# One 256-column pass for each token's product in the table of weights, with the low part of u on GpSimd

## The reference, cut to what matters

```python
idx = jnp.take_along_axis(cand_i, pos, axis=-1)      # i1 * 128 + i2
gate = jax.nn.softmax(top_s, axis=-1)
hid = jnp.einsum('td,thkd->thk', xb, u_tab[ib]).astype(jnp.float32)
coef = (jax.nn.gelu(hid, approximate=False) * gb).astype(xb.dtype)
y = jnp.einsum('thk,thkd->td', coef, v_tab[ib])
```

## Time and profile before

| | before |
|---|---|
| median of 3 runs | 2252.08 us |
| profiled execution, in all | 2255.32 us |
| its span | 2253.5 us |
| TensorE busy | 2013.6 us (89%) |
| VectorE busy | 1570.8 us (70%) |
| ScalarE busy | 1002.6 us (44%) |
| GpSimd busy | 125.6 us (6%) |
| table stage | about 1630 to 1881 us of the span |
| expert stage | about 1882 to 2241 us |

### The profile page before, as it was taken

How to read it: one execution, slowest core, us unless ns; L and a number is a source line. 1 busy time by engine, 2 the same in 40 slices (tenths; PEclk the granted TensorE clock), 3 DMA queues, 4 the chain that set the end, 5 groups by cost and what they waited for, 6 DMA issues and landing times. The chain is left out here.

```text
span 2253.5 us, 40848 instructions
## 1 busy us (share of the span) xinstructions
PE 2013.6 (89%) x16472; PEld 1805.2 (80%) x16472; DVE 1570.8 (70%) x2622; ACT 1002.6 (44%) x1669; POOL 125.6 (6%) x109
## 2 busy tenths in 40 slices
PE   8877799988779996998788888899899999999996
PEld 4875599968559894878777868899899998888885
DVE  3658778867559886776566565589977776667665
ACT  2515444335553343323344553445456665454453
POOL 1000000000230001530000300000000000000000
PEclk9967999989789998998899988999999999999998
DMA  7672578835137882314000025477555555777775
GB/s 262 229 165 82 196 291 319 310 119 187 59 134 282 304 299 70 119 57 151 1 4 4 2 86 189 150 230 216 181 170 176 176 176 196 240 242 244 241 241 179
DMA packets 185264, 393.24 MB, mean 174 GB/s; under 512 B 14826, under 2 KB 130154, under 8 KB 173546
## 3 DMA queue, kind: packets, MB, share of 16 engines
q1 hardware_dynamic: 166642, 373.83, 49.1%
q10 hardware_dynamic: 18434, 16.79, 2.2%
HBM read 371.17 MB, written 19.40 MB: 173 GB/s over the span
## 5 line engine op out<-in xcount | busy, mean ns | idle before, releaser
L1319 ACT CAST experts_v_hi<-peer_v 128x1024 fp32r<-128x1024 f32 x128 | 134.3, 1050 | 175.8 <-PE experts_py L1309 174.7
L1516 PE MATMUL ffn_pa<-all_h_hi,ffn_u_hi 128*128 128x256 f32 x704 | 199.4, 283 | 7.1 <-DVE ffn_u_lo L1581 7.0
L1305 PE MATMUL experts_py<-experts_v_hi,experts_c_hi 128*128 128x512 f32 x512 | 200.4, 391 | 5.3 <-DVE experts_c_lo L1350 5.3
L1306 PE MATMUL experts_py<-experts_v_lo,experts_c_hi 128*128 128x512 f32 x512 | 200.1, 391 | 0.0
L1517 PE MATMUL ffn_pa<-all_h_lo,ffn_u_hi 128*128 128x256 f32 x704 | 198.2, 282 | 0.0
L1518 PE MATMUL ffn_pa<-all_h_hi,ffn_u_lo 128*128 128x256 f32 x704 | 198.2, 281 | 0.0
L1309 PE MATMUL experts_py<-experts_v_hi,experts_c_lo 128*128 128x512 f32 x512 | 158.4, 391 | 0.0
L3148 PE MATMUL table_pa<-all_h_hi,table_u_hi 128*128 128x256 f32 x512 | 151.1, 295 | 7.6 <-DVE table_u_lo L3116 7.6
L1344 DVE TENSOR_TENSOR experts_v_lo<-peer_v,experts_v_hi 128x1024 fp32r<-128x1024 f32 x128 | 155.9, 1218 | 0.6 <-ACT experts_v_hi L1319 0.6
L3070 PE MATMUL route_pa<-all_h_hi,route_u_hi 128*128 128x256 f32 x512 | 146.5, 286 | 8.8 <-DVE route_u_lo L2955 8.8
L3071 PE MATMUL route_pa<-all_h_lo,route_u_hi 128*128 128x256 f32 x512 | 145.7, 285 | 0.0
(11 more groups left out here) (586 smaller groups left out, 5828.9 us busy)
## 6 DMA issues: line engine op xcount, KB each, us to landing
peer_v<-in_peer_v SPq DMA_DIRECT2D x128, 512.0 KB, 3.4
ffnw_u<-in_ffn_columns SPq DMA_DIRECT2D x44, 1024.0 KB, 7.9
ffn_ada_w<-in_ada_w SPq DMA_DIRECT2D x40, 1024.0 KB, 5.4
route_u<-in_peer_u SPq DMA_DIRECT2D x64, 512.0 KB, 3.8
table_u<-in_peer_u SPq DMA_DIRECT2D x64, 512.0 KB, 3.3
ffnw_v<-in_ffn_rows SPq DMA_DIRECT2D x44, 512.0 KB, 8.7
peer_kept<-hid_kept SPq DMA_DIRECT2D x128, 128.0 KB, 3.4
l1w_w<-in_diff_w_in SPq DMA_DIRECT2D x12, 1024.0 KB, 5.1
```

The lines of the kernel that those rows point to most:

```text
L1305: pe.matmul(py[:, 2 * t + n, :], c_hi[:, b, part], v_hi[:, r, cols], start=start, stop=False)
L1306: pe.matmul(py[:, 2 * t + n, :], c_hi[:, b, part], v_lo[:, r, cols], start=False, stop=False)
L1516: pe.matmul(out, u_hi[:, b, cols], h_hi[:, c, :], start=(c == 0), stop=False)
```

## The change

- `first` and `second` become float32r. The gates are rounded at the start of the stage to a high part; high part and remainder are kept in PSUM (`gates`). `second` gets 256 columns for each token: the one-hot row times the high part, and beside it times the low part. A token's product is one matmul of 256 columns, whose two halves are summed later.
- `one_hot` on VectorE is now: `equal` (comparison of the second keys, whole quad), `first` (the same for the first keys), `second` (a product of `equal` with the gates, 1024 elements).
- `products` goes by halves of a quad, with 5 PSUM banks for halves in place of 4 for quads. ScalarE copies the low half of each product into `table` (`low_table`), and VectorE adds the high half from PSUM (`store`), one step behind `one_hot`.
- `low_u` moves from VectorE to GpSimd.
- `table` lies as [key 1, token, key 2], so the copies write it densely, and `weigh` in `experts` reads it with a stride of 128 values.
- `hid` has 2 buffers in place of 3.

```diff
-                dve.tensor_tensor(coef[:, i % 2, :], feed_h.slot(i), table[:, i, :], ALU.mult).then_inc(weighed, 1)
+                dve.tensor_tensor(coef[:, i % 2, :], feed_h.slot(i), table[:, :, i], ALU.mult).then_inc(weighed, 1)
...
-    ring, hots, banks = 3, 2, 4
+    ring, kept, hots, banks = 3, 2, 2, 5
...
-        first = st.sb("first", [P, hots, per, NKEYS])
-        second = st.sb("second", [P, hots, per, NKEYS])
+        first = st.sb("first", [P, hots, per, NKEYS], F32R)
+        equal = st.sb("equal", [P, per, NKEYS])
+        second = st.sb("second", [P, hots, per, 2, NKEYS], F32R)
...
-        hid = st.sb("hid", [P, ring, S])
-        psum = st.ps("psum", [P, banks, CW])
+        hid = st.sb("hid", [P, kept, S])
+        psum = st.ps("psum", [P, banks, per // 2, 2, NKEYS])
+        gates = st.ps("gates", [P, 2, S])
...
+        @block.gpsimd
+        def _(pool):
+            for j in range(late):
+                pool.wait_ge(u_hi_ready, j + 1)
+                pool.tensor_tensor(u_lo[:, j % 2, :], u[:, j % ring, :], u_hi[:, j % 2, :].bitcast(F32), ALU.subtract
+                                   ).then_inc(u_split, 1)
...
             def one_hot(i):
                 b = i % hots
+                at = slice(i * per, (i + 1) * per)
+                keys = k["iota"][:].unsqueeze(1).broadcast_to(wide)
+                if i >= 1:
+                    dve.wait_ge(hot, i)
+                dve.tensor_tensor(equal[:], chosen[:, 1, at].unsqueeze(2).broadcast_to(wide), keys, ALU.is_equal
+                                  ).then_inc(equal_ready, 1)
                 if i >= hots:
-                    dve.wait_ge(product, i - hots + 1)
-                wide = [P, per, NKEYS]
-                at = slice(i * per, (i + 1) * per)
-                dve.tensor_tensor(first[:, b], chosen[:, 0, at].unsqueeze(2).broadcast_to(wide),
-                                  k["iota"][:].unsqueeze(1).broadcast_to(wide), ALU.is_equal)
-                for j in range(per):
-                    key, gate = [chosen[:, c, i * per + j:i * per + j + 1] for c in (1, 2)]
-                    last = dve.tensor_scalar(second[:, b, j, :], k["iota"][:], key, gate, ALU.is_equal, ALU.mult)
-                last.then_inc(hot, 1)
-
-            for i in range(max(late, quads)):
-                if i < late:
-                    low_u(i)
-                if i < quads:
-                    one_hot(i)
+                    dve.wait_ge(product, 2 * (i - hots + 1))
+                dve.tensor_tensor(first[:, b], chosen[:, 0, at].unsqueeze(2).broadcast_to(wide), keys, ALU.is_equal)
+                dve.wait_ge(equal_ready, i + 1)
+                dve.tensor_tensor(second[:, b], equal[:].unsqueeze(2).broadcast_to(pair),
+                                  gates[:, :, at].rearrange("p a t -> p t a").unsqueeze(3).broadcast_to(pair),
+                                  ALU.mult).then_inc(hot, 1)
+
+            def store(i):
+                for half in range(2):
+                    n = 2 * i + half
+                    dve.wait_ge(copied, n + 1)
+                    at = i * per + half * per // 2
+                    to = table[:, at:at + per // 2, :]
+                    dve.tensor_tensor(to, to, psum[:, n % banks, :, 0, :], ALU.add).then_inc(stored, 1)
+
+            high = second[:, 0].rearrange("p t a n -> p (t a n)")[:, 0:S]
+            dve.tensor_copy(high, chosen[:, 2, :]).then_inc(gate_ready, 1)
+            dve.wait_ge(gate_ready, 1)
+            dve.tensor_copy(gates[:, 0, :], high.bitcast(F32)).then_inc(gate_ready, 1)
+            dve.tensor_tensor(gates[:, 1, :], chosen[:, 2, :], high.bitcast(F32), ALU.subtract).then_inc(gate_ready, 1)
+            dve.wait_ge(gate_ready, 3)
+            for i in range(quads):
+                one_hot(i)
+                if i >= 1:
+                    store(i - 1)
+            store(quads - 1)
...
-                if i >= banks:
-                    pe.wait_ge(stored, i - banks + 1)
-                for j in range(per):
-                    last = pe.matmul(psum[:, i % banks, j * P:(j + 1) * P], first[:, b, j, :], second[:, b, j, :],
-                                     start=True, stop=True)
-                last.then_inc(product, 1)
+                for half in range(2):
+                    n = 2 * i + half
+                    if n >= banks:
+                        pe.wait_ge(stored, n - banks + 1)
+                    for m in range(per // 2):
+                        j = half * per // 2 + m
+                        last = pe.matmul(psum[:, n % banks, m].rearrange("p a n -> p (a n)"), first[:, b, j, :],
+                                         second[:, b, j].rearrange("p a n -> p (a n)"), start=True, stop=True)
+                    last.then_inc(product, 1)
...
-            def store(i):
-                act.wait_ge(product, i + 1)
-                act.copy(table[:, :, i * per:(i + 1) * per].rearrange("p n t -> p t n"),
-                         psum[:, i % banks, :].rearrange("p (t n) -> p t n", t=per)).then_inc(stored, 1)
+            def low_table(i):
+                for half in range(2):
+                    n = 2 * i + half
+                    at = i * per + half * per // 2
+                    act.wait_ge(product, n + 1)
+                    act.copy(table[:, at:at + per // 2, :], psum[:, n % banks, :, 1, :]).then_inc(copied, 1)
```

More of the change, by code:

```diff
@@ L3084, in peer_table @@
     late = columns.shape[0] - early
-    ring, hots, banks = 3, 2, 4
+    ring, kept, hots, banks = 3, 2, 2, 5
     h_hi, h_lo = k["h_hi"], k["h_lo"]
     with Stage(nc, "table") as st:
-        first = st.sb("first", [P, hots, per, NKEYS])
-        second = st.sb("second", [P, hots, per, NKEYS])
+        first = st.sb("first", [P, hots, per, NKEYS], F32R)
+        equal = st.sb("equal", [P, per, NKEYS])
+        second = st.sb("second", [P, hots, per, 2, NKEYS], F32R)
         u = st.sb("u", [P, ring, D])
         u_hi, u_lo = (st.sb(n, [P, 2, D], F32R) for n in ("u_hi", "u_lo"))
-        hid = st.sb("hid", [P, ring, S])
-        psum = st.ps("psum", [P, banks, CW])
+        hid = st.sb("hid", [P, kept, S])
+        psum = st.ps("psum", [P, banks, per // 2, 2, NKEYS])
+        gates = st.ps("gates", [P, 2, S])
         pa = st.ps("pa", [P, 2, CW])
         u_loaded = [st.sem(f"u_loaded{i}") for i in range(ring)]
-        hid_kept_done = [st.sem(f"hid_kept{i}") for i in range(ring)]
-        hot, product, stored, u_hi_ready, u_split, rows_ready, acted = (
-            st.sem(n) for n in ("hot", "product", "stored", "u_hi_ready", "u_split", "rows_ready", "acted"))
+        hid_kept_done = [st.sem(f"hid_kept{i}") for i in range(kept)]
+        gate_ready, equal_ready, hot, product, copied, stored, u_hi_ready, u_split, rows_ready, acted = (
+            st.sem(n) for n in ("gate_ready", "equal_ready", "hot", "product", "copied", "stored", "u_hi_ready", "u_split", "rows_ready", "acted"))
         block = st.block()
@@ L3108, in _ @@
                 feed.begin(sp)
-            for b in range(ring):
-                sp.wait_ge(hid_kept_done[b], 16 * len(range(b, late, ring)))
+            for b in range(kept):
+                sp.wait_ge(hid_kept_done[b], 16 * len(range(b, late, kept)))
+        @block.gpsimd
[4 more added lines that the diff above has]
+                                   ).then_inc(u_split, 1)
@@ L3112, in _ @@
         @block.vector
         def _(dve):
[L3114 to L3117, removed]
+            wide = [P, per, NKEYS]
+            pair = [P, per, 2, NKEYS]
             def one_hot(i):
                 b = i % hots
-                if i >= hots:
-                    dve.wait_ge(product, i - hots + 1)
-                wide = [P, per, NKEYS]
-                at = slice(i * per, (i + 1) * per)
-                dve.tensor_tensor(first[:, b], chosen[:, 0, at].unsqueeze(2).broadcast_to(wide),
-                                  k["iota"][:].unsqueeze(1).broadcast_to(wide), ALU.is_equal)
-                for j in range(per):
-                    key, gate = [chosen[:, c, i * per + j:i * per + j + 1] for c in (1, 2)]
-                    last = dve.tensor_scalar(second[:, b, j, :], k["iota"][:], key, gate, ALU.is_equal, ALU.mult)
-                last.then_inc(hot, 1)
@@ L3178, in gate_tile @@
                 act.wait_ge(rows_ready, j + 1)
-                if j >= ring:
-                    act.wait_ge(hid_kept_done[j % ring], 16 * (j // ring))
-                act.activation(hid[:, j % ring, :], pa[:, j % 2, 0:S], ACT.Gelu).then_inc(acted, 1)
+                if j >= kept:
+                    act.wait_ge(hid_kept_done[j % kept], 16 * (j // kept))
+                act.activation(hid[:, j % kept, :], pa[:, j % 2, 0:S], ACT.Gelu).then_inc(acted, 1)
             def keep_tile(j):
                 act.wait_ge(acted, j + 1)
-                act.dma_start(hid_kept[early + j], hid[:, j % ring, :]).then_inc(hid_kept_done[j % ring], 16)
-            def store(i):
-                act.wait_ge(product, i + 1)
```

(9 more changed lines are left out.)

## The result

The changed kernel takes 2241.03 us, the median of 4 runs (2239.59 to 2243.99), against 2253.39 for the kernel before (4 runs, 2250.52 to 2256.25). The ratio is 0.9947, with a 95% interval from 0.9934 to 0.9961: 12.4 us faster, between 8.8 and 14.9. Forecast were 2239.5 us and 12.7 us less.

What follows compares the result with a forecast made beforehand. TensorE's matmuls bound the table stage at 3.767 us per tile. 62 tiles at 3.55 save 13.5 us, the start gives back 1.2, the end saves 0.4: 12.7 off 2252.1, rounded to 2239.5 us, range 2228 to 2252.

Steps and rivals of the forecast that it cites:

- TensorE's part: Table stage: four tokens' table matmuls hold TensorE 0.48 us in place of 0.90; were TensorE the bound, 3.35 us per tile.
- The ring: Table stage: two `u_hi` buffers pass between GpSimd, TensorE and ScalarE; one turn takes 7.03 us, a tile 3.52.
- The turns: Table stage: GpSimd's subtraction and VectorE's `equal` and `first` exclude each other when reading SBUF, 3.38 to 3.62 us per tile.
- The 3.55: Table stage: us per tile taken for GpSimd-VectorE alternation and the two-buffer `u_hi` cycle together, down from 3.767.
- the 0.1 to 0.2 that was named as a sign: Table stage: TensorE would idle 0.1 to 0.2 us per tile, released by GpSimd, if the forecast was right.
- VectorE, 3.00 us in issue: Table stage: VectorE's comparisons, `second` and two adds take 3.00 us of a 3.52 us tile, not the bound by itself.
- Start and end: Table stage: first low part on GpSimd delays the start by 1.2 us; last `keep_tile` DMA goes out 0.4 us sooner.
- `weigh`: Expert stage: strided reads lengthen it from 418 ns to 0.56 to 0.68 us, at zero cost up to 1.25 us.
- TensorE at 3.35: Table stage: TensorE stays the bound at 3.35 to 3.44 us per tile, 2227 to 2233 us in all; 12 in 100.
- The slower case: Table stage: comparisons and both hand-overs cost over 1.35 us; at 4.00 us per tile, 2267 us in all; 6 in 100.
- rival 2: Table stage: GpSimd-VectorE alternation costs more than the rows, 3.65 to 3.77 us per tile, 2246 to 2253 us; 11 in 100.
- rival 3: Table stage: slower kernel, 4.00 us per tile, 14 us lost, 2.0 with the start, 2267 us; 6 in 100.

## Why the prediction was right

- **TensorE's part, 0.90 to 0.48 us per quad.** Right: the matmuls start 0.12 us apart, and 3.360 us per tile where nothing else bounds it (3.35 forecast).
- **The ring, 7.03 us for two tiles.** Right, to the hundredth: 1706.24 - 1699.21 = 7.03, and 3.516 per tile over the stage. Its parts are right too: the Gelu and the cast are 0.28 us apart (1704.84 and 1705.12), and the cast and GpSimd 1.12 (1706.24), as in the earlier trace rows. That it is the bound is shown by the keys in PSUM (nothing held, same tile), the cast ahead (3.42), and the third buffer with the keys in PSUM (3.36).
- **The turns, 3.38 to 3.62.** Right in kind and in range: 3.42 by GpSimd's tight gap (1.01 + 2.41) and 3.43 by its growing durations. They lie below the ring and cost the changed kernel nothing. The 3.55 that I took for both together was 0.03 too much; that is the largest mis-sized term, 62 x 0.03 = 2 us. The waits of 6.4 us for GpSimd's low part come to 0.1 us per tile, the lower end of the 0.1 to 0.2 that was named as a sign.
- **VectorE, 3.00 us in issue.** Right: its 60.00 of 60 is held time, as VectorE takes 87 of 100 without holds.
- **Start and end.** At the start the low part of tile 2 begins 15.0 us after the last copy of `chosen` (1646.54 - 1631.5), against 14.3 (1642.92 - 1628.6): +0.7, not +1.2. From the last low part to the first `weigh` it is 8.3 us instead of 9.2: -0.9, not -0.4.
- **`weigh`.** 629 ns, between 560 and 680, and hidden: the expert tile is 2.72 us as before, and the layout alone changes nothing.
- **The sum.** From the last copy of `chosen` to the first `weigh` the change saves 15.5 us (253.3 to 237.8): 61 x 0.251 = 15.3 in the tiles, 0.7 lost at the start and 0.9 saved at the end. Forecast for this were 12.7, so three terms were too pessimistic by 2.8 us together: the 3.55, the start and the end. That 12.4 came out all the same is luck. In the profiled execution the stage begins 2.9 us later than before, and nothing ahead of it is part of the change. 2.5 of the 2.9 us lie in the inversion of the delta-net layer (`dninv`): from the first to the last start of its matmuls at L2410 it takes 114.9 us in the kernel before and 117.4 in the changed one, and 111.6 in the one with three buffers and the keys in PSUM, at a granted clock of 0.99 to 1.00 in all three. Over the profiled executions of all kernels the last copy of `chosen` starts anywhere from 1620.9 to 1633.3 us. What makes the stages ahead differ stays open.
- **The rivals.** TensorE at 3.35 needed a longer ring and the keys out of SBUF. The slower case (4.00 us, from the point at which pair and hand-overs pass 1.35 us) did not come here, but such a price appeared under another edit: with three buffers GpSimd got in between the comparisons, and the tile took 4.24 us. The mechanism that I gave it, both comparisons at full length and two hand-overs of 0.10, was not the one. What opens it is GpSimd's request falling between them, which rival 2 had as "once in a while". The "2.0 with the start" in rival 3's sum stands on no row: 62 x (4.00 - 3.767) = 14.4, with 1.2 for the start and 0.4 for the end, gives its 2267.

## What to carry to other kernels

When the busiest engine gets less to do, work out each ring (buffers x tile against one whole turn, all its hand-overs counted) and take its longest: here two buffers and 7.03 us set the new tile, to the hundredth. A ring that is slightly slower than a shared resource's round can be what keeps that resource in order; before a buffer is added, see whether two engines read SBUF in turns, and take one's operand out to PSUM first. And an engine's busy share says nothing of its load where its instructions can be held: compare the median duration with the shortest.

## What was unexpected of the hardware

- A GpSimd instruction's recorded duration includes its wait for the shared reading: 2.40 us bare, 2.47 to 2.94 when its request came during a VectorE comparison. A request that VectorE makes 0.06 us too late (1669.55 against 1669.49) costs it the whole of the other's instruction.
- Engines that take turns in 3.43 us and are asked every 3.36 don't settle at 3.43. They drifted for eight tiles, then GpSimd got in between VectorE's two comparisons, and a tile took 4.24 us from there on.
- A tensor_scalar with one SBUF tensor and two scalars read from SBUF was held as well (339 ns in the median, 2436 at most), once for each quad.
- Reading 256 float32 values 512 bytes apart took 629 ns on VectorE where dense ones took 418: 0.82 ns more for each.
